# Moving a shared on-chip region by 64 bytes so that it begins at a multiple of 128

## The reference, cut to what matters

```
# first block
px = hx @ w_in;  y = g_f * (fourier(f) @ w_fourier) + g_a * (att @ w_mla_o)
x = x + g1 * (y @ w_out)
x = x + g2 * square(relu(h2 @ w_up)) @ w_down
# second block
y = sigmoid(ga) * (oa @ w_a_out) + sigmoid(gb) * (ob @ w_b_out)
x = x + y @ w_o
x = x + memory_attention(...) @ w_mo
x = x + (silu(gate) * up) @ w_down;  out = rmsnorm(x, norm_final)
```

## Time and profile before

| | |
|---|---|
| device time, three runs | 2299.1, 2306.67, 2311.11 us, median 2306.67 |
| profiled execution, first to last instruction | 2299.4 us; no device time of its own is given for it |
| TensorE, matmuls | 2214.0 us busy (96%), 11528 of them |
| TensorE, weight loads | 1834.8 us busy (80%) |
| VectorE / ScalarE / GpSimd | 895.4 / 830.7 / 882.8 us busy (39 / 36 / 38%) |
| mean granted TensorE clock | 0.983 of full speed |
| DMA | 205.89 MB, mean 90 GB/s |

### The profile page before, as it was taken

One profiled execution on the slowest core, in us unless ns is written; L12 is line 12 of the kernel. 1 busy time (PEld: TensorE's weight loads), 2 busy tenths in 40 slices (PEclk: granted clock), 3 DMA queues, 4 the chain that ended last, 5 costly groups with the idle time before them and its releaser, 6 DMA issues.

```text
span 2299.4 us, 28706 instructions
## 1 busy us (share of the span) xinstructions
PE 2214.0 (96%) x11528; PEld 1834.8 (80%) x11528; DVE 895.4 (39%) x1411; ACT 830.7 (36%) x1208; POOL 882.8 (38%) x640
## 2 busy tenths in 40 slices
PE   6999999999999989999999999999999999999998
PEld 3777778878888868979797878788888988888886
DVE  2457855441211246564747420505143344222102
ACT  3355433232322335242424323535323443222212
POOL 0335943434444434030321244132254625444442
PEclk9999999999999999989999999999999999999999
DMA  6412333422233233020301122131332412222321
GB/s 235 147 55 68 116 103 112 163 73 92 92 102 99 92 108 101 20 74 6 105 20 55 37 92 92 38 110 38 110 110 92 147 56 91 92 91 97 104 91 55
DMA packets 179968, 205.89 MB, mean 90 GB/s; under 512 B 3364, under 2 KB 170768, under 8 KB 179472
## 3 DMA queue, kind: packets, MB, share of 16 engines
q1 hardware_dynamic: 176912, 195.17, 26.2%
q10 hardware_dynamic: 2944, 9.15, 1.1%
HBM read 198.01 MB, written 6.29 MB: 89 GB/s over the span
## 4 chain that ended last, share of the span: by engine, by line
PE 83%; DVE 6%; ACT 2%; POOL 2%; issue 1%; DMA 1%; DVEq 0%; ACTq 0%; SPq 0%
PE ps L2071 20%; PE ps L2073 20%; PE ps L2072 20%; PE ps L2180 4%; PE ps L2587 2%; PE ps L2392 2%; PE ps L2600 2%; POOL w_lo L688 2%; PE ps L2671 2%; PE ps L2688 1%; PE ps L2358 1%; PE ps L2118 1%; PE ps L2120 1%; PE ps L2119 1%; ACT w_hi L760 1%
## 5 line engine op out<-in xcount | busy, mean ns | idle before, releaser
L688 POOL TENSOR_TENSOR w_lo<-raw,w_hi 128x512 fp32r<-128x512 f32 x586 | 780.6, 1364 | 1353.0 <-ACT w_hi L760 1353.0
L2071 PE MATMUL ps<-h_hi,w_hi 128*128 128x512 f32 x1384 | 560.4, 405 | 12.9 <-DVE h_lo L1407 4.8
L2073 PE MATMUL ps<-h_hi,w_lo 128*128 128x512 f32 x1384 | 545.3, 394 | 0.0
L2072 PE MATMUL ps<-h_lo,w_hi 128*128 128x512 f32 x1384 | 544.2, 393 | 0.0
L760 ACT ACTIVATE w_hi<-raw 128x2048 fp32r<-128x2048 f32 x150 | 285.7, 1905 | 371.0 <-PE ps L2073 363.6
L2071 PEld LDWEIGHTS ps<-h_hi,w_hi 128*128 128x128 f32 x1384 | 263.0, 190 | 74.3 <-issue 10.5
L2073 PEld LDWEIGHTS ps<-h_hi,w_lo 128*128 128x128 f32 x1384 | 262.8, 190 | 56.9
L2072 PEld LDWEIGHTS ps<-h_lo,w_hi 128*128 128x128 f32 x1384 | 263.2, 190 | 52.4 <-issue 1.2
L2071 PE MATMUL ps<-g_hi,w_hi 128*128 128x512 f32 x256 | 101.0, 394 | 0.0
L2073 PE MATMUL ps<-g_hi,w_lo 128*128 128x512 f32 x256 | 100.4, 392 | 0.0
L2072 PE MATMUL ps<-g_lo,w_hi 128*128 128x512 f32 x256 | 99.4, 388 | 0.0
(11 more groups left out here) (417 smaller groups left out, 3856.4 us busy)
## 6 DMA issues: line engine op xcount, KB each, us to landing
raw<-w_in SPq DMA_DIRECT2D x48, 1024.0 KB, 5.2
raw<-w_down SPq DMA_DIRECT2D x27, 1024.0 KB, 5.1
raw<-ada_w SPq DMA_DIRECT2D x24, 1024.0 KB, 5.2
raw<-w_gate_up SPq DMA_DIRECT2D x22, 1024.0 KB, 5.0
raw<-w_up SPq DMA_DIRECT2D x16, 1024.0 KB, 5.4
raw<-w_mkv SPq DMA_DIRECT2D x8, 1024.0 KB, 5.4
raw<-w_out SPq DMA_DIRECT2D x4, 1024.0 KB, 5.5
xT<-bias_band SPq DMA_DIRECT2D x2, 2048.0 KB, 9.9
```

Of the source, the lines that this page charges most:

```text
L688: ins = nc.gpsimd.tensor_tensor(w_lo[:, split_at[u] % 2, cols], raw[:, u % 2, cols], w_hi[:, split_at[u] % 2, cols].bitcast(F32), ALU.subt ...
L2071: T.matmul(out_, wh, hi, start=start, stop=False, skip_group_check=True)
L2072: T.matmul(out_, wh, lo, start=False, stop=False, skip_group_check=True)
L2073: return T.matmul(out_, wl, hi, start=False, stop=stop, skip_group_check=True)
```

## The change

The base of the region is rounded up to the next multiple of 128.

```diff
@@ -125,7 +125,7 @@
     sq2 = fixed("sq2", [P, 2, S])
     acc = fixed("acc", [P, S])
     tmp2 = fixed("tmp2", [P, 2, S])
-    BASE = at[0]
+    BASE = (at[0] + 127) // 128 * 128
 
     class Region:
 
```

## The result

The changed kernel takes 2309.22 us (median of 13 runs, 2305.26 to 2319.87), the kernel before 2302.53 us (13 runs, 2297.91 to 2311.11). The ratio is 1.0035 with a 95% interval of 1.0022 to 1.0048, so it is slower by 5 to 11 us. The forecast was 4.2 us less than the 2306.67 of the three runs before, 2302.5. That this equals the median of the 13 runs before is chance.

The account below looks back on a forecast made before the run. TensorE, with matmuls in flight for 96% of the span, was taken to bound the kernel. The terms 3.6 + 1.2 - 0.6 = 4.2 us came off 2306.67, giving 2302.5 us; the range for 8 in 10 was 2294 to 2312.

Parts of the forecast that it names:

- What bounds the kernel, and that only TensorE's pace could matter: Whole kernel: TensorE has matmuls in flight for 96% of the span and is 83% of the chain.
- The comparison inside the kernel, 226.9 ns on `h` and 229.0 on the region's tiles: MLP phases of 192 equal matmuls: 43.57 us on `h`, 43.97 on `g`, with the streamed tile's place as the difference left.
- I take it that at a multiple of 128 a region tile goes at `h`'s pace: Streamed 512-column tiles: nine phases of 192 save 3.6 us, the 528 matmuls on `s` 1.2 us.
- Rival 2: Streamed and stationary reads hinder each other: 6.1 ns more on 2256 back-to-back matmuls, 13.8 us slower, 2321 us; chance 0.08.
- The opposite sign of the token phases: Matmuls streaming 256 columns: 119.9 ns with `h` stationary, 113.8 with `m`, so the tile at a multiple of 128 is slower.
- rival 1: The place does nothing; `h`'s pace belongs to something the change leaves: 2306.7 us; chance 0.22.
- Stationary `m`: Token units with `m` stationary, 256 columns streamed: slowed to 119.9 ns per matmul, costing 0.6 us, bounds 0 and 0.9.
- The wide `m` matmuls, put at 0: Matmuls of 256 columns on `m`, standing between waits for `w_lo`: 0 us.
- `fm` and `at` at 0: 192 matmuls at about 400 to 430 us: 0, as a faster matmul only waits longer for load, ScalarE and GpSimd.
- Delta rule's tiles, ScalarE, VectorE, transfers at 0: Plain float32 matmuls, the other engines' accesses and region transfers: 0 us each; transfers bounded by 0 and 0.9 less.
- rival 3: More than forecast: 4.8 us saved and the delta rule's matmuls gain 4.3 us as well, 2297.6 us; chance 0.10.
- The page's rule: Accesses pay only on crossing to a new 16-byte line; by that alone the change is worth nothing, 2306.7 us.

Follow-up runs that it names:

- the sweep: Computation left out, matmuls alone, 96 for each of 33 placements of streamed against stationary tile: 229.0 ns at +64, 233.3 at +128, 226.8 at +256.

## Why the prediction was wrong, point by point

- **What bounds the kernel, and that only TensorE's pace could matter:** right. The steps of the float32r matmuls add up to 9.2 us, and the difference at equal clock is 9.0.
- **The comparison inside the kernel, 226.9 ns on `h` and 229.0 on the region's tiles:** right as measured, and that it is a matter of address and not of other engines was right too; the sweep has the same two numbers with nothing else running.
- **"I take it that at a multiple of 128 a region tile goes at `h`'s pace":** this is the step that failed. `h` was quick because it stands level with the weights modulo 256, not because of its own address. The change put the region 128 bytes out of step instead of 64, and that costs 233.3 ns. The term of the sum was -4.8 us for 2256 matmuls; it measured +8.6.
- **Rival 2 was the mechanism, and it was set aside for a wrong reason.** Its own sign came, over 44.5 us for a phase on `g` (44.79). It said that how the streamed and the stationary read stand to each other might count, and named the residues modulo 256. The argument against it, that "in bytes from a multiple of 128 the new pair is the one of `h`", took 128 for the period. Nothing in the rows spoke for that period: the one tile at a multiple of 128 was also the one at a distance of 0 modulo 256. Its price was borrowed from the token phases, 6.1 ns for each of the 2256, and came to 8.6 us / 2256 = 3.8 ns, up to 4.3 in a phase without waits. The rest of the way from 2321 to 2309 is that the three runs before had a median 4.1 us above that of the 13, and the clock. That 2309.22 lies within the 2294 to 2312 of the prediction is luck: that range was made for rivals 1 and 3 and the spread of the runs, and the change went the other way.
- **The opposite sign of the token phases** was noted, as support for rival 1. Held together with the earlier trace rows, where `h` is the quick tile when streamed and not the slow one, it spoke against a simple rule on one tile's own address, and so for rival 2 as much as for rival 1. That was the row to give rival 2 more than 0.08. It didn't decide the matter: those matmuls have 256 columns, and by the sweep they go by other numbers.
- **Stationary `m`:** the sign was right. 118.6 ns in place of 113.3 (forecast 119.9), and 0.4 us more over the four units from first to last, waits included (forecast 0.6 more). The wide `m` matmuls, put at 0, took 0.2 more.
- **`fm` and `at` at 0:** not quite. Their matmuls slowed down like the others, and the waits for `w_lo` took up only a part of it (0.4 to 0.8 us more for the stretch).
- **Delta rule's tiles, ScalarE, VectorE, transfers at 0:** right for the groups of the earlier trace rows, which moved by 2 ns at most. So rival 3, a gain in the delta rule's matmuls, falls. Of the transfers, `x_in` took 9.7 us instead of 10.8, but 10.0 at the base 130112 too, which is again 64 beyond a multiple of 128; the masks took 4.4 as before.
- **Rival 1, the place does nothing:** falls, since the region's own pace went from 229.0 to 233.3 ns and, at another base, to 226.7.
- **The page's rule:** The Trainium skill, "SBUF — State Buffer", section "Door 1: The DMA port swizzle", says that an access pays when it crosses to a new line of 16 bytes. If that were all that counts, there would have been no change. It isn't: both bases are whole numbers of such lines and the paces differ, and by the sweep a shift of exactly one line costs 5 ns at 512 columns.

## What to carry to other kernels

"Aligned" is a statement about two operands. For float32r matmuls of 512 columns in a kernel bound by TensorE, place the streamed tiles and the weights at the same residue modulo 256 bytes (226.7 ns against 229 to 238), and time a phase from first start to first start to see it; the duration in a row or the busy share hardly shows it. When the only good example in a trace differs from the others in two ways, say which of them the forecast leans on, and price the other.

## What the runs showed of the hardware that was not expected

- A float32r matmul of 512 columns takes 226.7, 228.9, 232.3 to 233.4 or 233.4 ns at a distance of 0, 64, 128 or 192 bytes modulo 256 between streamed and stationary operand, and up to 238.0 at other distances (+4 bytes). It repeats with 256, and moves with the stationary tile.
- With 256 columns the sweep has another order: 120.0, 117.8, 118.6, 113.3. It is no rule by the distance alone: at 64 and at 192 both 113.3 and 117.8 ns were seen, and at 128 both 118.6 and 120.0. With 128 columns there is no difference (111.6 to 111.7), and plain float32 at 512 columns shows none either (429.2).
- The time falls by about 1.5 us for each 0.001 of mean granted clock, so executions whose clocks differ by 0.002 differ by as much as many a change is worth.
